# The recurrent stage in chunks of 64 tokens instead of 32, each solved over two 32-token halves

## The chip, the cores and the metric

The kernel runs on one core of one Trainium2 chip. The metric is the device time of one execution in microseconds (us); below it is the median of the runs shown. The engines are named as in the profile: PE (TensorE matmul), PEld (its weight load), DVE (VectorE), ACT (ScalarE), POOL (GpSimd) and SP (SyncE, which here issues loads).

## The reference, cut to what matters

The kernel computes one step of a hybrid decoder layer for a prompt of 2048 tokens and a small sample. Only the recurrence of its RWKV-7 branch for the prompt bears on the change: eight heads, each with a 64 x 64 state `s` that every token reads and rewrites.

```
def step(s, inp):
    r_t, w_t, k_t, v_t, kk_t, kka_t = inp
    s_kk = einsum('bhvk,bhk->bhv', s, kk_t)
    s = s * w_t[:, :, None, :] - s_kk[..., None] * kka_t[:, :, None, :] + v_t[..., None] * k_t[:, :, None, :]
    return s, einsum('bhvk,bhk->bhv', s, r_t)
s_final, ys = lax.scan(step, s0, xs)          # over the tokens
y = (y - mean) * rsqrt(var + eps) * lnx_g + lnx_b   # per head, and a bonus term and a gate behind it
```

Within a chunk of tokens the scan is solved in closed form: with products between the chunk's keys (the grams, masked to a triangle), the corrections u of all its tokens solve a unit triangular system, so that u is an inverse times a right-hand side q. Then the state moves on by one chunk, and the outputs y come from the state and from the grams.

## The kernel before, in words

Stages run one after another: the front, a sample start, the attention of the prompt and of the sample, `stage_rwkv` (L979), the merge. The change is in `stage_rwkv`, apart from constant masks made in the front.

The stage walks over 16 blocks of 128 tokens in a software pipeline. In round n each engine does, for different blocks: the recurrence of block n, the inverses of block n+1 (grams L1323, then five rounds of squaring L1346), the features of block n+2 (decays, keys, transposes), the inputs of block n+3, and the normalisation and output of block n-1. The order of each engine's work in a round is written out by hand, and semaphores tie the engines to one another.

A block has four chunks of 32 tokens. Heads are spread over the array in pairs: the four 32-row and 32-column tiles of TensorE each hold the tokens of one pair p, and e picks one of its two heads. For each chunk:

- `open_chunk` (L1349): gram times v (L1359), state times keys (L1363) into q, half of keys times values (L1368). It waits for the copy of the y before it, since q and y lie in the same PSUM tile.
- ACT copies q (`take_q`, L1588); `solve` (L1372): the other half of keys times values (L1377), inverse times q (L1385).
- DVE copies u (`take_u`, L1796); `close_chunk` (L1389): rates times u into the state (L1396, L1405), the state's part of y (L1400), the grams' parts of y (L1410, L1414).
- DVE adds the new state (`next_state`, L1804); ACT copies y (`take_y`, L1595).

Between these, PE does the other blocks' work: grams, `low_rank` (L1255, L1256), squares, transposes (`turn_values` L1278, `turn_keys` L1287, `turn_rates` L1294, `norms` L1272, `turn_y` L1310), `bonus_sums` (L1301), `key_sums` (L1265). On ACT the decays need two activation tables, so in every round a block stands there without a break: a table load, two roots, a table load, the exponentials, and three copies out of PSUM (L1550 to L1568). On DVE the norm's `centre_y` (L1818) reads two operands from SBUF; `mask` (L1764) writes the masked grams. On POOL `first_product` (L1176) adds the identity to the triangle, `shifted` (L1157) multiplies the token differences, `receptance` (L1190) forms the operand of the bonus sums.

Of the kernel before, what the change touches and what calls it, by code (L numbers as in the profile page):

```python
# [22 lines left out]
P = 128  # L23
# [137 lines left out]
def stage_front(nc, t, k, h_t, z_t, z_s, w_idx, w_idx_s, scores, part):  # L161
# [3 lines left out]
    with Stage(nc, "fro") as s:  # L165
# [128 lines left out]
        def _(pool):  # L294
# [19 lines left out]
            for c, lt, le, gt in ((32, k.m_lt, k.m_le, k.m_gt), (4, k.s_lt, k.s_le, k.s_gt)):  # L314
# [8 lines left out]
            chain.link(pool.memset(k.chunk_start[:, :].rearrange("p (b c) -> p b c", c=32)[:, :, 0:1], 0.0))  # L323
# [655 lines left out]
def stage_rwkv(nc, t, k, z_t, y_t, weights):  # L979


    C = 32
    NC = P // C
    BLK = 2 * NC
    with Stage(nc, "rwk") as s:
# [4 lines left out]
        mask4, eye = s.sb("mask4", [P, 4 * C]), s.sb("eye", [P, C])  # L990
        rheads = s.sb("rheads", [P, 4, P])
        g_tok = s.sb("g_tok", [P, 2, HD])
# [4 lines left out]
        kr, sq, th_w, th_a, mix, cum, kk, rk, bs = (s.sb(n, E) for n in ("kr", "sq", "th_w", "th_a", "mix", "cum", "kk", "rk", "bs"))  # L997
# [7 lines left out]
        v_tok = [s.sb(f"v_tok{i}", [P, NC, 2 * HD]) for i in range(3)]  # L1005
        k_tok = [s.sb(f"k_tok{i}", [P, NC, 2 * HD]) for i in range(2)]
        b_tok = [s.sb(f"b_tok{i}", [P, NC, 2 * HD]) for i in range(2)]
        gram = [s.sb(f"gram{i}", [P, 2, NC, 2, 2, C]) for i in range(2)]
        ta = [s.sb(f"ta{i}", [P, BLK, 2, C]) for i in range(2)]
        pw = [s.sb(f"pw{i}", [P, BLK, C]) for i in range(2)]  # L1010
        inv = [s.sb(f"inv{i}", [P, BLK, C]) for i in range(2)]
        q_tok = [s.sb(f"q_tok{i}", [P, 2, HD]) for i in range(2)]
        u_tok = [s.sb(f"u_tok{i}", [P, 2, HD]) for i in range(2)]
        state = [s.sb(f"state{i}", [P, 2, 2, HD]) for i in range(2)]
        kept = s.sb("kept", [P, 2, 2, HD])
        y_tok = [s.sb(f"y_tok{i}", [P, NC, 2, HD]) for i in range(2)]
        y_sum, y_var = s.sb("y_sum", [P, 8]), s.sb("y_var", [P, 8])
        y_c, y_sq, y_n, y_g = (s.sb(n, [P, 8, HD]) for n in ("y_c", "y_sq", "y_n", "y_g"))
        y_2, g_th, gate, y_out = (s.sb(n, E) for n in ("y_2", "g_th", "gate", "y_out"))
        bias = [s.sb(f"bias{i}", E) for i in range(3)]  # L1020
        s_out = s.sb("s_out", [HD, 4, P])
# [17 lines left out]
        q_ok, q_copied, u_ok, u_copied, o_half, o_ok, st, keep, y_ok, y_copied = (  # L1039
            s.sem(n) for n in ("q_ok", "q_copied", "u_ok", "u_copied", "o_half", "o_ok", "st", "keep", "y_ok", "y_copied"))  # L1040
# [23 lines left out]
        def rows(p):  # L1064
            return slice(C * p, C * p + C)

        def half_of(e):
            return slice(HD * e, HD * e + HD)

        def tokens(c):  # L1070
            return slice(C * c, C * c + C)

        def lower(g):

            return g[:, :, :, 1, 0, :].rearrange("p e c t -> p (e c) t")

        HEADS = [(p, e) for p in range(4) for e in range(2)]
# [6 lines left out]
        def _(sp):  # L1084
# [13 lines left out]
            for m in range(4):  # L1098
# [4 lines left out]
                if m == 0:  # L1103
                    for p in range(4):
                        sp.dma_start(g_tok[rows(p), :, :].rearrange("p e v -> p (e v)"),
                                     t["lnx_g"][:, P * p:P * p + P].to_broadcast([C, P])).then_inc(g_in, 16)
            for n in range(NT):
                sp.wait_ge(u_ok, NC * n + 1)
                if n and n + 3 < NT:
                    load_z(n + 3, 1, Z_PIECES[1][2])  # L1110
                weights.load_piece(sp, 3 * n)
                sp.wait_ge(o_ok, NC * n + 1)
                if n >= 2:
                    sp.wait_ge(gate_ok, n - 1)
                load_gate(n, slice(0, 2))
                sp.wait_ge(u_ok, NC * n + 2)
                load_gate(n, slice(2, 4))
                sp.wait_ge(o_ok, NC * n + 2)
                weights.load_piece(sp, 3 * n + 1)
                if n + 4 < NT:  # L1120
                    free_z(n + 4, 0)
                    load_z(n + 4, 0, Z_PIECES[0][0])
                    sp.wait_ge(u_ok, NC * n + 3)
                    load_z(n + 4, 0, Z_PIECES[0][1])
                    sp.wait_ge(o_ok, NC * n + 3)
                    load_z(n + 4, 0, Z_PIECES[0][2])
                    sp.wait_ge(u_ok, NC * n + 4)
                    free_z(n + 4, 1)
                    load_z(n + 4, 1, Z_PIECES[1][0])
                    sp.wait_ge(o_ok, NC * n + 4)  # L1130
                    load_z(n + 4, 1, Z_PIECES[1][1])
                else:
                    sp.wait_ge(u_ok, NC * n + 4)
# [12 lines left out]
        def _(pool):  # L1146
# [24 lines left out]
            def first_product(m):  # L1171

                pool.wait_ge(masked, 2 * m + 2)
                if m:
                    pool.wait_ge(acc_ok, 4 * m)
                pool.tensor_tensor(ta[1][:, :, 1, :], lower(gram[m % 2]), eye[:, None, :].to_broadcast([P, BLK, C]), ALU.add).then_inc(acc1_ok, 1)  # L1176
# [24 lines left out]
            def scale_y(e):  # L1201
                pool.wait_ge(yn_ok, e + 1)
                if e:
                    pool.wait_ge(y_turned, e)
                pool.tensor_tensor(y_g[:, :, :].rearrange("p (c e) v -> p c (e v)", e=2), y_n[:, :, :].rearrange("p (c e) v -> p c (e v)", e=2),
                                   g_tok[:, :, :].rearrange("p e v -> p (e v)")[:, None, :].to_broadcast([P, NC, P]), ALU.mult).then_inc(yg_ok, 1)

            def put_out(e):
                pool.wait_ge(y2_ok, e + 1)
                pool.wait_ge(gate_ok, e + 1)  # L1210
                if e:
                    pool.wait_ge(stored, 16 * e)
# [5 lines left out]
            for n in ROUNDS:  # L1218
                if there(n):
                    keep_state(n, 0)  # L1220
                if there(n + 1):
                    end_keys(n + 1)
                if there(n + 1):
                    first_product(n + 1)
                if there(n + 3):
                    shifted(n + 3, 0)
# [4 lines left out]
                if there(n):  # L1231
                    keep_state(n, 2)
# [4 lines left out]
                if there(n):  # L1237
                    keep_state(n, 3)
                if there(n + 2):
# [6 lines left out]
        def _(pe):  # L1246
# [28 lines left out]
            def turn_values(m):  # L1275
                pe.wait_ge(thw_ok, m + 1)
                for c in range(NC):
# [1926 lines left out]
```

## Time and profile before

| what | us |
|---|---|
| median of 3 runs | 3555.86 (3547.37 to 3557.55) |
| span of the profiled execution | 3554.5 |
| of it before the stage | 2087.5 |
| of it in the stage, 2087.5 to 2733.0 | 645.5 |
| of it behind the stage | 821.5 |
| PE busy in the stage | 525.4 |
| DVE, ACT, POOL busy in the stage | 339.9, 345.0, 245.7 |
| mean granted TensorE clock in the stage, as a share of full | 0.67 |

The span is the trace's own length; the profiled execution lies 1.4 us under the median of the runs. A granted clock of 1 is 2.4 GHz, of 0.5 it is 1.2 GHz; a share between the two is a mix in time. A row of the timeline names a run of equal instructions, its start, its length and the wait ahead of it; the trace counts two matmuls for each call here, so that a group of 8 calls has x16. Starts of consecutive groups on PE, one taken from the next, give what a group costs, since their modelled ends overlap.

### The profile page before, as it was taken

Reading aid. Unit: us, or ns where it says so; the run is one execution under the profiler, and the core shown is the slowest. Engines: PE = TensorE matmul, PEld = TensorE weight load, DVE = VectorE, ACT = ScalarE, POOL = GpSimd, SP = SyncE. Lnnn points to the kernel's source line nnn. Section 1 sums busy time; section 2 is a strip of 40 time slices with the busy share of each in tenths; the row PEclk is TensorE's granted clock in tenths of the full one; section 3 lists DMA queues with packets and bytes.
Section 4 is the critical chain, followed back from the end, with each engine's and each line's share of the span. In section 5 each row is a group of like instructions: output and inputs, shape, how many; then the busy total and the mean of one; then the engine's idle time right before and its main releaser. Section 6 shows DMA issues by size and latency. Waiting matters only on the chain. (4 is left out here: it accounts for less than half of the span.)

```text
span 3554.5 us, 73586 instructions
## 1 busy us (share of the span) xinstructions
PE 3287.0 (92%) x29368; PEld 1981.7 (56%) x29368; DVE 2139.6 (60%) x4326; ACT 1100.1 (31%) x2345; POOL 525.2 (15%) x764
## 2 busy tenths in 40 slices
PE   8999999999999999699999658888886899999998
PEld 4544445555555555466666437667665555555553
DVE  2018889999999999377766544546553344432211
ACT  4136650000000000255555245555552111111211
POOL 3330000000000000211011333433432000000000
PEclk9999999999999999699999766666776999999999
DMA  5241111111111111332111641222212511121110
GB/s 157 74 106 50 42 46 56 56 56 56 55 61 55 56 56 50 88 80 53 42 37 29 213 122 41 51 48 52 53 28 68 167 63 57 62 75 63 48 39 24
DMA packets 215719, 233.95 MB, mean 66 GB/s; under 512 B 28665, under 2 KB 190900, under 8 KB 214884
## 3 DMA queue, kind: packets, MB, share of 16 engines
q1 hardware_dynamic: 147832, 110.00, 11.4%
q0 software_dynamic: 23696, 59.79, 5.9%
q10 hardware_dynamic: 43868, 59.62, 4.8%
q8 instruction: 232, 3.80, 0.5%
q14 instruction: 91, 0.75, 0.1%
HBM read 158.69 MB, written 70.63 MB: 65 GB/s over the span
## 5 line engine op out<-in xcount | busy, mean ns | idle before, releaser
L409 PE MATMUL fro_acc<-h_t,fro_w 128*128 128x416 f32 x3280 | 1175.0, 516 | 0.0
L409 PEld LDWEIGHTS fro_acc<-h_t,fro_w 128*128 128x128 f32 x3280 | 614.7, 190 | 542.9 <-issue 535.9
L692 DVE TENSOR_SCALAR_CACHE_REDUCE fro_work<-scores,fro_real 128x384 uint8<-128x384 f32 (+6 forms) x462 | 656.2, 1474 | 2.1
L516 ACT ACTIVATE fro_out<-fro_acc 128x416 f32<-128x416 f32 (+3 forms) x230 | 118.1, 513 | 794.0 <-PE fro_acc L409 711.2
L2134 PE MATMUL mrg_po<-mrg_wo,mrg_mrg 128*128 128x512 f32 (+1 forms) x544 | 238.2, 596 | 5.1 <-DVE mrg_mrg L2239 5.1
L3070 DVE CUSTOM_DVE_ANT_0 att_seen<-att_ps,scores 128x512 f32<-128x512 f32 (+3 forms) x320 | 181.4, 608 | 100.8 <-PE att_ps L2956 100.3
L2166 PE MATMUL mrg_pg<-mrg_wg,mrg_x_t 128*128 128x512 f32 (+1 forms) x544 | 236.3, 592 | 0.0
L658 DVE SCALAR_TENSOR_TENSOR scores<-fro_work,w_idx,scores 128x512 f32<-128x512 f32 (+3 forms) x280 | 188.0, 671 | 39.2 <-ACT fro_work L573 12.2
L2134 PEld LDWEIGHTS mrg_po<-mrg_wo,mrg_mrg 128*128 128x128 f32 (+1 forms) x544 | 101.1, 186 | 139.2 <-issue 133.8
L3040 ACT ACTIVATE att_seen<-att_seen,att_shift 128x128 f32<-128x128 f32 (+15 forms) x128 | 152.7, 1195 | 84.1 <-DVE att_shift L3078 84.1
L2956 PE MATMUL att_ps<-att_kt,att_qt 64*128 64x512 f32 (+3 forms) x640 | 159.7, 588 | 14.2 <-POOL att_sel L2927 14.2
L573 ACT ACTIVATE fro_work<-fro_wk 128x512 f32<-128x512 f32 (+3 forms) x320 | 144.5, 539 | 90.8 <-PE fro_wk L482 89.9
L2166 PEld LDWEIGHTS mrg_pg<-mrg_wg,mrg_x_t 128*128 128x128 f32 (+1 forms) x544 | 100.5, 185 | 125.5 <-issue 124.9
L2992 PEld LDWEIGHTS att_po<-att_prob_t,att_v 128*64 128x64 f32 x2176 | 116.9, 137 | 91.3 <-issue 59.4
L2969 PE MATMUL att_pt<-ident,att_seen 128*128 128x128 f32 x1088 | 157.0, 284 | 6.2 <-ACT att_seen L3040 6.0
L2992 PE MATMUL att_po<-att_prob_t,att_v 128*64 128x128 f32 x2176 | 155.3, 282 | 0.0
L2085 POOL DMA_DIRECT2D mrg_m_in<-z_t x72 | 51.2, 711 | 676.3 <-DVE mrg_mrg L2239 673.7
L2444 POOL MEMSET sst_w2a<- 128x1024 f32 x1 | 1.0, 951 | 995.6 <-POOLq L100 995.6
L2101 PE MATMUL mrg_br<-mrg_y_in,wr 128*128 128x256 f32 (+2 forms) x576 | 127.9, 366 | 19.0 <-DMA mrg_y_in<-y_t 14.4
L2314 DVE SCALAR_TENSOR_TENSOR mrg_th<-mrg_th,mrg_pw 128x1024 f32<-128x1024 f32 (+1 forms) x17 | 20.8, 1221 | 204.2 <-ACT mrg_th L2216 204.2
L2329 DVE RECIPROCAL mrg_rstd<-mrg_rstd 128x1 f32<-128x1 f32 (+1 forms) x17 | 2.8, 163 | 225.6 <-ACT mrg_rstd L2202 225.6
L2969 PEld LDWEIGHTS att_pt<-ident,att_seen 128*128 128x128 f32 x1088 | 118.7, 143 | 35.0 <-issue 29.8
(441 smaller groups left out, 4667.4 us busy)
## 6 DMA issues: line engine op xcount, KB each, us to landing
z_t<-fro_out ACTq DMA_DIRECT2D x180, 208.0 KB
fro_w<-in_w_in SPq DMA_DIRECT2D x41, 512.0 KB, 4.1
mrg_m_in<-z_t POOLq DMA_DIRECT2D x56, 256.0 KB, 3.5
scores<-in_cache_kv POOLq DMA_DIRECT2D x108, 128.0 KB, 3.2
rwk_zi<-z_t SPq DMA_DIRECT2D x80, 129.0 KB, 2.6
z_t<-fro_out ACTq DMA_DIRECT2D x45, 192.0 KB
scores<-in_x_prompt SPq DMA_DIRECT2D x16, 512.0 KB, 8.2
mrg_x<-in_x_prompt SPq DMA_DIRECT2D x16, 512.0 KB, 3.6
```

The lines of the kernel that those rows point to most:

```text
L409: last = pe.matmul(acc[e % 2][:, 0:CW], w[block_no % 3][:, kk, :], h_t[:, kk, CW * g:CW * g + CW], start=(kk == 0), stop=(kk == KD - 1))
L573: act.activation(rel[m % 8][:, 0:width], wk[m % 6][:, 0:width], ACT.Relu).then_inc(relued, 1)
L658: ins = dve.scalar_tensor_tensor(o, rel[m % 8][:, 0:width], wh, o, ALU.mult, ALU.add)
L692: chain.mark(dve.tensor_scalar(junk[b % 2][:, 0:n], scores[:, c:c + n], realf[:, b:b + 1], None, op, ALU.add, accum_out=count[:, b:b + 1]))
L2101: last = pe.matmul(br[:, at % 2, W * a:W * a + m], w[:, c, d * P:(d + 1) * P], y_in[g % 2][:, a, c, 0:m], start=(c == 0), stop=(c == 3))
L2134: last = pe.matmul(po[0:n, 512 * h:512 * h + 512], mrg[g % 2][:, c, o:o + n], wo[:, c, 512 * h:512 * h + 512], start=(c == 0), stop=(c == ...
L2166: last = pe.matmul(pg[0:n, 512 * h:512 * h + 512], x_t[:, c, 0:n], wg[:, c, 512 * h:512 * h + 512], start=(c == 0), stop=(c == KD - 1))
L2956: last = pe.matmul(ps[z % 2][e][:, 0:width], qt[b % 2][w, hh, :], kt[w, 512 * sl:512 * sl + width], start=True, stop=True)
L2969: last = pe.transpose(pt[i % 2][:, 256 * e + P * a:256 * e + P * a + P], seen[n % 3][e][:, P * kb:P * kb + P], k.ident[:, :])
L2992: last = pe.matmul(po[b % 2][64 * e:64 * e + 64, P * hh:P * hh + P], v[:, kb, 64 * e:64 * e + 64], prob_t[i % 4][:, 256 * e + P * a:256 * ...
L3040: act.activation(row, row, ACT.Exp, bias=shift[n % 3][:, e:e + 1], scale=scale, accum_out=total[b % 2][:, 4 * e + hh:4 * e + hh + 1]).then ...
L3070: dve.tensor_tensor_reduce(seen[n % 3][e][:, 512 * sl:512 * sl + width], ps[z % 2][e][:, 0:width], scores[:, c:c + width], 1.0, -3.4e38, A ...
```

## The change

A block now has two chunks of 64 tokens. Each chunk's triangular system is solved by forward substitution over two halves of 32 tokens, so that only 32 x 32 inverses are kept: solve the first half, multiply it by the off-diagonal block of the gram (`carry`), add that to the second half's right-hand side, solve the second half. The five rounds of squaring have as many matmuls as before. Groups that were spread over 32-wide tiles now use 64 x 64 tiles, all four of them (state, keys times values, rates times u) or the two on the diagonal (grams times v and u); the two solves and the carry use 32 x 32 tiles, two at a time. The grams come in two parts, one for each chunk, with 128 moving columns each. The gram part of q for the next chunk is issued at the end of `close_chunk` (`begin_q`).

```
-    C = 32
+    C, H = 64, 32
     NC = P // C
-    BLK = 2 * NC
+    BLK = 2 * NC * 2
...
             def first_product(m):
...
+                for i, (x, h) in enumerate(FOURTHS):
+                    w = fourth(x, h)
+                    pool.tensor_tensor(ta[1][w, :, 1, :], lower(gram[m % 2])[w, :, sub(h)], eye[w, None, :].to_broadcast([H, BLK, H]), ALU.add)\
+                        .then_inc(acc1_ok, 1)
+                    pool.wait_ge(acc1_ok, 4 * m + i + 1)
...
+            def grams(m, c):
...
+                for i in range(2):
+                    for p2, x, e in HEADS:
+                        p = 2 * p2 + x
+                        last = pe.matmul(zz[half_of(x), e, 256 * p2 + P * i:256 * p2 + P * i + P], kbz[half_of(e), i, p, tokens(c)],
+                                         ar[m % 3][half_of(e), p, c, :, :].rearrange("p a c -> p (a c)"), start=True, stop=True)
...
+            def solve(n, c, h):
...
+                for p2, e, x in ALONG:
+                    w = fourth(x, h)
+                    last = pe.matmul(qy[w, e, P + 64 * p2:P + 64 * p2 + 64], inv[n % 2][w, block_no(e, c, p2), :],
+                                     q_tok[m % 2][w, e, p2, :], start=False, stop=True, skip_group_check=True)
                 last.then_inc(u_ok, 1)
+            def carry(n, c):
+                m = NC * n + c
+                pe.wait_ge(u_copied, 4 * m + 2)
+                for p2, e, x in ALONG:
+                    w = fourth(x, 0)
+                    last = pe.matmul(qy[fourth(x, 1), e, 64 * p2:64 * p2 + 64], lower(gram[n % 2])[w, block_no(e, c, p2), sub(1)],
+                                     u_tok[m % 2][w, e, p2, :], start=False, stop=True, skip_group_check=True)
+                last.then_inc(carried, 1)
+            def take_in(n, c):
+                m = NC * n + c
+                now, u = state[m % 2], u_tok[m % 2]
+                pe.wait_ge(u_copied, 4 * m + 4)
...
+            def take_carry(n, c):
+                m = NC * n + c
+                act.wait_ge(carried, m + 1)
+                for x in range(2):
+                    w = fourth(x, 1)
+                    act.activation(q_tok[m % 2][w, :, :, :].rearrange("p e b v -> p e (b v)"), qy[w, :, 0:P], ACT.Copy).then_inc(q_copied, 1)
...
+            def take_u(n, c, h):
...
+                for x in range(2):
+                    w = fourth(x, h)
+                    dve.tensor_copy(u_tok[m % 2][w, :, :, :].rearrange("p e b v -> p e (b v)"), qy[w, :, P:2 * P]).then_inc(u_copied, 1)
...
                 if norm:
                     sum_y(n - 1)
+                    centre_y(n - 1)
+                if inverse:
+                    mask(n + 1, 0)
                 if loop:
-                    take_u(n, 0)
+                    take_u(n, 0, 0)
```

Some tiles share memory now (rk with mix, y_n with y_c, y_g with y_sq, the gate with its tanh, y_out with y_2), with the waits that this asks for, and SP's loads are tied to other semaphores of the recurrence. The new order shows at three places.

On PE, from the close of a block's first chunk to the solve of the next, before (L1346 is the squares, L1363 state times keys):

```order
L1396 MATMUL rwk_oo<-rwk_u_tok,rwk_b_tok 64x64 x4
L1400 MATMUL rwk_qy<-rwk_state,rwk_ar 32x64 x8
L1405 MATMUL rwk_oo<-rwk_u_tok,rwk_b_tok 64x64 x4
L1410 MATMUL rwk_qy<-rwk_v_tok,rwk_gram 32x64 x8
L1414 MATMUL rwk_qy<-rwk_u_tok,rwk_gram 32x64 x8
L1359 MATMUL rwk_qy<-rwk_v_tok,rwk_gram 32x64 x8
L1363 MATMUL rwk_qy<-rwk_state,rwk_ar 32x64 x8
L1368 MATMUL rwk_oo<-rwk_v_tok,rwk_k_tok 64x64 x4
L1346 MATMUL rwk_zz<-rwk_gram,rwk_pw 32x32 x32
L1377 MATMUL rwk_oo<-rwk_v_tok,rwk_k_tok 64x64 x4
L1385 MATMUL rwk_qy<-rwk_q_tok,rwk_inv 32x64 x8
```

The same place after (L1423 to L1427 is `take_in`, L1435 to L1372 `close_chunk` with `begin_q`, L1386 and L1392 `open_chunk`, L1363 the squares, L1405 a half's solve, L1291 and L1300 transposes):

```order
L1291 MATMUL rwk_xx<-ident,rwk_vx 128x128 x4
L1423 MATMUL rwk_oo<-rwk_u_tok,rwk_b_tok 64x64 x8
L1427 MATMUL rwk_qy<-rwk_state,rwk_ar 64x64 x8
L1363 MATMUL rwk_zz<-rwk_gram,rwk_pw 32x32 x32
L1435 MATMUL rwk_qy<-rwk_v_tok,rwk_gram 64x64 x8
L1438 MATMUL rwk_qy<-rwk_u_tok,rwk_gram 64x64 x8
L1372 MATMUL rwk_qy<-rwk_v_tok,rwk_gram 64x64 x8
L1386 MATMUL rwk_qy<-rwk_state,rwk_ar 64x64 x8
L1392 MATMUL rwk_oo<-rwk_v_tok,rwk_k_tok 64x64 x8
L1363 MATMUL rwk_zz<-rwk_ta,rwk_pw 32x64 x32
L1405 MATMUL rwk_qy<-rwk_q_tok,rwk_inv 32x64 x8
L1300 MATMUL rwk_xx<-ident,rwk_kbt 128x128 x4
```

One group of the open (L1372, the gram part of q) has moved ahead of the place where it waits for the copy of y, and the square that stood between open and solve has a successor there; the state's groups stand ahead of the first square. On DVE, the start of a round before:

```order
L1811 TENSOR_REDUCE rwk_y_sum<-rwk_y_tok 128x8
L1796 COPY rwk_u_tok<-rwk_qy 128x128
L1764 TENSOR_TENSOR rwk_gram<-rwk_zz,rwk_mask 128x512 x2
L1804 TENSOR_TENSOR rwk_state<-rwk_oo,rwk_kept 128x256
L1772 STREAM_TRANSPOSE rwk_pw<-rwk_gram 128x256
L1818 SCALAR_TENSOR_TENSOR rwk_y_c<-rwk_y_sum,rwk_y_tok 128x512
L1796 COPY rwk_u_tok<-rwk_qy 128x128
L1707 TENSOR_SCALAR rwk_th_w<-rwk_th_w 128x512
```

and after (L1852 and L1858 are the norm's sum and `centre_y`, L1799 the mask, L1837 the copies of u):

```order
L1852 TENSOR_REDUCE rwk_y_sum<-rwk_y_tok 128x8
L1858 SCALAR_TENSOR_TENSOR rwk_y_c<-rwk_y_sum,rwk_y_tok 128x512
L1799 TENSOR_TENSOR rwk_gram<-rwk_zz,rwk_mask 128x512 x2
L1837 COPY rwk_u_tok<-rwk_qy 32x256 x2
L1799 TENSOR_TENSOR rwk_gram<-rwk_zz,rwk_mask 128x512 x2
L1837 COPY rwk_u_tok<-rwk_qy 32x256 x2
L1807 STREAM_TRANSPOSE rwk_pw<-rwk_gram 128x512
L1845 TENSOR_TENSOR rwk_state<-rwk_oo,rwk_kept 128x256
```

`centre_y` has moved from behind the first state to ahead of the masks and of all copies of u. On ACT, from the second table load on, before:

```order
L1541 ACT_TABLE_LOAD
L1541 ACTIVATE rwk_e_in<-rwk_cum 128x16x32
L1542 ACTIVATE rwk_e_neg<-rwk_cum 128x512
L1546 ACTIVATE rwk_p_end<-rwk_cum 128x16
L1556 ACTIVATE rwk_rnb<-rwk_nrm 128x512
L1562 ACTIVATE rwk_v_tok<-rwk_xx 128x512
L1568 ACTIVATE rwk_k_tok<-rwk_xx 128x512
L1595 ACTIVATE rwk_y_tok<-rwk_qy 128x128
L1576 ACTIVATE rwk_ta<-rwk_zz 128x8x32
L1588 ACTIVATE rwk_q_tok<-rwk_qy 128x128
```

and after (L1607 copies a square, L1626 is `take_carry`):

```order
L1572 ACT_TABLE_LOAD
L1572 ACTIVATE rwk_e_in<-rwk_cum 128x8x64
L1573 ACTIVATE rwk_e_neg<-rwk_cum 128x512
L1577 ACTIVATE rwk_p_end<-rwk_cum 128x8
L1587 ACTIVATE rwk_rnb<-rwk_nrm 128x512
L1593 ACTIVATE rwk_v_tok<-rwk_xx 128x512
L1607 ACTIVATE rwk_ta<-rwk_zz 128x8x32
L1599 ACTIVATE rwk_k_tok<-rwk_xx 128x512
L1626 ACTIVATE rwk_q_tok<-rwk_qy 32x256 x2
```

A copy of y and one of q stood behind the block; now the two copies of the carried half do.

## Rows read from the trace of the kernel before

**Rows 1.** Windows: length, busy PE PEld DVE ACT POOL, PEclk, DMA

```profile
2149.59:2701.59 552.00, 475.58 (x15136) 379.46 (x15135) 297.23 (x562) 295.33 (x796) 214.79 (x214) 0.70 0.18 44
2336.68:2375.45 38.77, 34.01 (x1020) 27.25 (x1016) 19.36 (x41) 21.01 (x57) 15.49 (x15) 0.65 0.21 50
2375.45:2411.59 36.14, 29.79 (x1020) 23.96 (x1016) 19.27 (x40) 20.88 (x57) 15.65 (x15) 0.76 0.22 53
```

**Rows 2.** Timeline of PE, lower level: start, length, work, idle before

```profile
2460.63 0.65 PE L1359 MATMUL rwk_qy<-rwk_v_tok,rwk_gram 32*32 32x64 f32 x16 [0.40 <-ACT rwk_y_tok L1595]
...
2462.02 1.08 PE L1346 MATMUL rwk_zz<-rwk_gram,rwk_pw 32*32 32x32 f32 x64
2463.03 0.49 PE L1377 MATMUL rwk_oo<-rwk_v_tok,rwk_k_tok 32*64 32x64 f32 x8
2463.45 0.65 PE L1385 MATMUL rwk_qy<-rwk_q_tok,rwk_inv 32*32 32x64 f32 x16
2464.03 1.11 PE L1278 MATMUL rwk_xx<-ident,rwk_vx 128*128 128x128 f32 x4
...
2466.17 0.49 PE L1396 MATMUL rwk_oo<-rwk_u_tok,rwk_b_tok 32*64 32x64 f32 x8
...
2467.41 0.65 PE L1410 MATMUL rwk_qy<-rwk_v_tok,rwk_gram 32*32 32x64 f32 x16
...
2468.26 1.81 PE L1346 MATMUL rwk_zz<-rwk_ta,rwk_pw 32*32 32x64 f32 x64
```

**Rows 3.** Timeline of PE, upper level; two groups behind a long wait

```profile
2447.00 0.34 PE L1396 MATMUL rwk_oo<-rwk_u_tok,rwk_b_tok 32*64 32x64 f32 x8
...
2448.29 0.76 PE L1346 MATMUL rwk_zz<-rwk_ta,rwk_pw 32*32 32x32 f32 x64
...
2643.12 0.43 PE L1359 MATMUL rwk_qy<-rwk_v_tok,rwk_gram 32*32 32x64 f32 x16 [0.40 <-ACT rwk_y_tok L1595]
...
2644.02 0.37 PE L1346 MATMUL rwk_zz<-rwk_gram,rwk_pw 32*32 32x32 f32 x19
...
2645.84 0.34 PE L1377 MATMUL rwk_oo<-rwk_v_tok,rwk_k_tok 32*64 32x64 f32 x8
...
2646.47 0.66 PE L1278 MATMUL rwk_xx<-ident,rwk_vx 128*128 128x128 f32 x4
...
2653.69 0.43 PE L1359 MATMUL rwk_qy<-rwk_v_tok,rwk_gram 32*32 32x64 f32 x16 [3.12 <-ACT rwk_y_tok L1595]
...
2654.43 0.49 PE L1368 MATMUL rwk_oo<-rwk_v_tok,rwk_k_tok 32*64 32x64 f32 x8
```

**Rows 4.** Waits of 2150:2720: total us, times, longest us

```profile
PE rwk_qy L1359 <- ACT rwk_y_tok L1595: 32.0, 32, 3.1
...
PE rwk_zz L1323 <- DVE rwk_nrm L1718: 9.0, 12, 1.1
...
PE rwk_xx L1287 <- issue: 8.6, 5, 3.4
...
PE rwk_oo L1377 <- issue: 0.7, 1, 0.7
```

**Rows 5.** Timeline of ACT: block of table loads, copies behind it

```profile
2426.44 1.28 ACT L1550 ACT_TABLE_LOAD   x1
...
2431.14 0.57 ACT L1562 ACTIVATE rwk_v_tok<-rwk_xx 128x512 f32<-128x512 f32 x1
...
2432.09 0.27 ACT L1595 ACTIVATE rwk_y_tok<-rwk_qy 128x128 f32<-128x128 f32 x1
```

**Rows 6.** DVE: lines L1818, L2530 (min/median/max ns); timeline

```profile
L1818 DVE SCALAR_TENSOR_TENSOR rwk_y_c<-rwk_y_sum,rwk_y_tok x16: 682/1530/5040, 2192.1 to 2723.3; 128x512 f32<-128x512 f32 x16
...
L2530 DVE COPY sst_tok<-sst_pb x3: 679/679/679, 1474.0 to 1477.1; 32x512 f32<-32x512 f32 x3
...
2459.99 3.37 DVE L1818 SCALAR_TENSOR_TENSOR rwk_y_c<-rwk_y_sum,rwk_y_tok 128x512 f32<-128x512 f32 x1
```

**Rows 7.** Timeline of POOL beside that centre_y

```profile
2459.12 1.67 POOL L1157 TENSOR_TENSOR rwk_pm<-rwk_zi,param 128x896 f32<-128x896 f32 x1
```

More of the change, by code:

```diff
@@ L1222, in _ @@
                     end_keys(n + 1)
+                if there(n + 3):
+                    shifted(n + 3, 0)
                 if there(n + 1):
                     first_product(n + 1)
[L1225 to L1226 removed]
                 if there(n):
@@ L1349, in open_chunk @@
             def open_chunk(n, c):
                 m = NC * n + c
-                g, now = gram[n % 2], state[c % 2]
-                if c == 0:
-                    pe.wait_ge(v_ok, n + 1)
-                    pe.wait_ge(b_ok, n + 1)
                 if m:
                     pe.wait_ge(y_copied, m)
-                for e in range(2):
-                    for p in range(4):
-                        pe.matmul(qy[rows(p), e, 0:64], g[rows(p), e, c, 0, 0, :], v_tok[n % 3][rows(p), c, half_of(e)], start=True, stop=False,
-                                  skip_group_check=True)
+                else:
+                    begin_q(0, 0).then_inc(y_ok, 1)
+                    pe.wait_ge(y_ok, 1)
@@ L1389, in close_chunk @@
             def close_chunk(n, c):
                 m = NC * n + c
-                g, now, u = gram[n % 2], state[c % 2], u_tok[m % 2]
-                pe.wait_ge(u_copied, m + 1)
-                pe.wait_ge(o_half, 3 * m + 2)
-                for p in (0, 1):
-                    for e in range(2):
-                        last = pe.matmul(oo[half_of(e), p % 2, 0:64], b_tok[n % 2][rows(p), c, half_of(e)], u[rows(p), e, :],
-                                         start=False, stop=True, skip_group_check=True)
@@ L1407, in close_chunk @@
[L1407 to L1415 removed]
+                pe.wait_ge(r_half, m + 1)
@@ L1424, in _ @@
                 if inverse:
-                    grams(n + 1)
+                    grams(n + 1, 0)
                 if loop:
-                    solve(n, 0)
+                    solve(n, 0, 0)
                 if features:
@@ L1430, in _ @@
                 if loop:
-                    close_chunk(n, 0)
-                    open_chunk(n, 1)
+                    carry(n, 0)
+                if inverse:
+                    grams(n + 1, 1)
+                if loop:
+                    solve(n, 0, 1)
+                if features:
+                    turn_values(n + 2)
+                if loop:
+                    take_in(n, 0)
                 if inverse:
@@ L1435, in _ @@
                 if loop:
-                    solve(n, 1)
-                if features:
-                    turn_values(n + 2)
+                    close_chunk(n, 0)
+                if loop:
+                    open_chunk(n, 1)
+                if inverse:
+                    square(n + 1, 1)
+                if loop:
+                    solve(n, 1, 0)
                 if inverse:
                     turn_keys(n + 1)
+                if features:
+                    norms(n + 2)
+                if loop:
+                    carry(n, 1)
+                if inverse:
+                    square(n + 1, 2)
+                if loop:
+                    solve(n, 1, 1)
+                if inverse:
+                    turn_rates(n + 1)
+                if inverse:
+                    square(n + 1, 3)
+                if loop:
+                    take_in(n, 1)
+                if features:
+                    bonus_sums(n + 2)
                 if loop:
```

413 lines of the change are left out of this document (191 added, 222 removed).

## The prediction

> **What bounds the kernel now.** Only the recurrent stage changes. I read the windows first: in fifteen rounds PE is busy for 475.6 of 552.0 us, DVE for 297, ACT for 295, POOL for 215 [rows 1]. A round is 36.8 us, of which PE is busy for 31.7; so PE bounds the stage, and what matters is its work, the level of its clock, and what it waits for. The clock decides as much as the work: a round of 38.77 us had a mean granted clock of 0.65, one of 36.14 us with the same number of matmuls had 0.76 [rows 1], so that a tenth of clock is worth about 2.4 us a round. Over the fifteen rounds the share was 0.70, a mix of the two levels, 1.2 and 2.4 GHz.
>
> Then the waits. PE stood still for 76.4 us in those rounds, 5.1 a round. The largest part is 32.0 us for the copy of y at the opening of a chunk, up to 3.1 us at a time, and 9.0 us at the grams [rows 4]; with the small ones it makes some 47 us, 3.1 a round. Seven rows of "issue", from 8.6 down to 0.7 us [rows 4], sum to 31.0 us, 2.1 a round.
>
> **PE's work in the chunks.** Costs go from start to start. At the lower level an open costs 2462.02 - 2460.63 = 1.39 us, a solve 2464.03 - 2463.03 = 1.00, a close 2468.26 - 2466.17 = 2.09 [rows 2]: 4.48, and 17.9 for four chunks. At the upper level these are 0.90, 0.63 and 1.29 [rows 3]: 2.82, and 11.3.
>
> No 64 x 64 tile is in this trace, so I build the new price from passes. The two y groups of the close take 2468.26 - 2467.41 = 0.85 us, that is 0.43 for 16 matmuls on four tiles, four deep: 0.107 us for one matmul of 64 columns. The square agrees: 64 on four tiles in 1.81, 16 deep [rows 2]. A group that is followed by another tile shape costs 0.15 more: the 16 of L1385 take 0.58 [rows 2]. A chunk now has ten groups of 16. Four lie on all four quadrants (4 deep, 0.43), six on two tiles (8 deep, 0.86): 4 x 0.43 + 6 x 0.86 = 6.9, and some five changes of shape, 0.75: 7.6 us, 15.2 a round. At the upper level I halve the pass, but keep a group of four tiles at 0.25 and a change at 0.10: 4 x 0.25 + 6 x 0.46 + 0.5 = 4.3, 8.6 a round. The chunks save 2.7 us a round at either level.
>
> The two parts of the grams issue 64 matmuls of 128 columns on four tiles, 16 deep at 0.214 us: 3.4, with two changes 3.7, against 16 x 0.107 + 0.15 = 1.9 before, where eight tiles worked: 1.8 us more, at the upper level 0.6 to 1.0 more. Squares keep their 160 calls. At the mix of levels in before PE's work falls by **1.4 us a round**. Bounds: if the quadrants go only two at a time, eight groups grow by 0.43 and the sum is +2.0; if neighbouring two-tile groups overlap where their tiles differ, as the solves and the squares might, half of twelve groups shrink by 0.43 and it is -4.0. I take the middle, because the 8 matmuls of L1377, which lie on two row and two column groups, take only 0.42 with their change of shape [rows 2], which is nearer to four at a time than to two.
>
> **Issue.** These waits sit behind dense runs of small matmuls. There are a quarter fewer of them now (some 756 a round instead of 1,012, by the calls in the code), and each one streams longer. Between nothing and the whole 2.1 us I take **-1.2 us a round**.
>
> **The new waits.** Forward substitution puts two hand-overs into a chunk where there was one: u copied by DVE, carry, q copied by ACT, solve, u copied again. Each copy is two instructions on 32 partitions. No such tile of 256 elements was in before; 32 partitions with 512 took 679 ns [rows 6], as long as 128 would, so I take 0.42 for 256, between 0.30 and 0.52: 0.84 a pair. Place by place, for the mix of levels:
> - The second chunk's open stands right behind the close and waits for a copy of 512 elements, 0.57 [rows 5], with its signal 0.75.
> - ACT's block lasts 2432.09 - 2426.44 = 5.65 us [rows 5]. Before, the third open waited for the y copy behind it. Now `norms` and the second `carry` stand there: the norms' operand is ready some 4.8 us after the block's start, and PE has a square (1.8), a solve (0.9) and four transposes (1.0) to do, 3.7 in all at the lower level and 2.1 at the upper: a wait of 1.0 to 2.7. The carry then waits for u, which DVE copies only behind the power that needs a square copied at the block's end: 1.5. Together 3.0.
> - `take_in` of the first chunk waits for a pair of copies, 0.84, with four transposes beside them: 0.5.
> - Bonus sums and key sums keep their feeding chains on DVE, POOL and ACT, while PE arrives sooner: 1.0 and 0.9.
> - The first carry: `centre_y` and a mask stand ahead of u's copy now, with `low_rank` on PE as cover: 0.4.
>
> That is 6.6 us a round against 3.1: **+3.5**, with 4.5 and 9 as ends. Edits priced at nothing: POOL's `first_product` in four steps with waits of their own has half the elements of a `shifted` (1.67 us for 896 [rows 7]) in all its steps together, some 2 us, and the close and open ahead of square 1 cover it; if that cover is gone it costs 0.7 a round. The transposes of 512 instead of 256 elements, the shared tiles and SP's new semaphores lie beside PE's work; late loads would show at the gate or at `shifted`, each of which has a round in hand.
>
> **The clock.** At the same clock the sum would be -1.4 - 1.2 + 3.5 = +0.9 us a round, a loss. What turns it is the level. In before it rose where PE worked without a pause through wide matmuls: behind bonus sums and transposes a whole close ran in 1.29 us [rows 3]. It fell behind the long waits: after one of 3.12 us the open began at the upper level, and its third group already took 0.49 instead of the 0.34 that a group of that tile takes at the upper level [rows 3]. Now the longest waits are split into shorter ones, and a chunk is fewer, longer streams with 10 shape changes a round instead of about 32. I expect a share of 0.78 instead of 0.70, which at 2.4 us a tenth is **-1.9 us a round**. This is the least certain term, between +1.2 (0.65) and -3.0.
>
> **Sum.** -1.4 - 1.2 + 3.5 - 1.9 = -1.0 a round, -16 over sixteen rounds. Filling and draining the pipeline, where the longer grams and the two-step chunk stand alone, costs some 2. The profiled execution of 3554.5 us lies 1.4 under the median, so I add to the median: 3555.9 - 14 = **3541**.
>
> **Rivals.**
> 1. The clock does not rise. More and longer gaps at norms, carry and bonus sums reset it as the 3.12 us wait did. At 0.70 the sum is 0.9 x 16 + 2 = +16: 3572; at 0.65, 1.2 a round more, 3591. It decides from 0.74 on downward (0.9 - 1.0). For it speaks that PE waits twice as long in all; against it that the single waits are shorter than 3.1. The Trainium skill, page "TensorE: Matmul & The Clock Gate", section "HAM oscillation — how this bites in real kernels", says that idle gaps between bursts of matmuls put the clock back each time; the row of the 3.12 us wait agrees, and by that rule this rival, not the forecast, would hold, with its 3572 to 3591.
> 2. `centre_y`, now ahead of u's first copy, becomes the hand-over that PE waits for. It took 682 ns at best, 1,530 in the median and 5,040 at worst; in the timeline one took 3.37 us, beside POOL work that began before it [rows 6, 7]. At a round's start POOL has the bias and output products to do. At 3.4 us instead of 1.5 the first carry waits 2 us more: 3541 + 32 = 3573; it decides above about 2 us. The Trainium skill, page "Advanced Engine Details and Errata", section "GPSIMD Details", says that POOL shares a read and a write interface with DVE, and that DVE instructions with two SBUF inputs conflict with it; the spread of 682 to 5,040 ns agrees.
> 3. Better than forecast: copies of 0.30 and two-tile groups that overlap, together 2 us a round: 3509.
> 4. The waits take the whole gain, as one that was hidden on ACT appears on PE: 3555.
>
> **Chances.** Forecast 0.38, its own range 3528 to 3556; rivals 0.22, 0.10, 0.20 and 0.10. A measurement of this kernel tells apart about 0.3%, 10.7 us. Faster than 3545.2: rival 3 and two thirds of the forecast, 0.45. Within it: the rest of the forecast and rival 4, 0.22. Slower than 3566.5: rivals 1 and 2, 0.33 with rounding. The range of 8 in 10 goes from rival 3 to rival 1 at 0.65: 3503 to 3592.
>
> **What would show it.** In the new profile: a round of 35.8 us; PE's groups on 64 x 64 quadrants at about 0.43 us at the lower level; issue under 1 us a round; waits of 6 to 7 us a round, with norms and the second carry first; a share of 0.78. A share at or below 0.72 is rival 1; a `centre_y` above 2 us and a first carry that waits over 2 us is rival 2; groups of 0.86 on four quadrants would break the work term.

## The result

The changed kernel took 3572.35 us (3569.54 to 3579.35) where the kernel before took 3553.3: a ratio of 1.0059, 95% interval 1.0043 to 1.0075. It is slower, by 19 us between the medians and by some 21 us by the ratio; the forecast was 14 us faster. The profiled execution of after has a span of 3576.2 us, 21.7 more than before's: 2.7 up to the first recurrent round, 12.0 in the fifteen rounds, 3.0 from there to the end of the stage, and 4.0 in the merge, which the change does not touch.

The windows view of after, one row for the fifteen rounds (length, busy us of PE, PEld, DVE, ACT and POOL with their counts, granted clock, DMA), answers to the first of [rows 1]:

```profile
2152.33:2716.30 563.97, 422.06 (x11304) 364.33 (x11296) 339.26 (x621) 307.26 (x795) 241.73 (x227) 0.76 0.17 43
```

PE is busy for 53.5 us less than before, and its clock's share rose from 0.70 to 0.76; but it stands still for 563.97 - 422.06 = 141.9 us instead of 76.4. The idle time ate the gain and 12 us more. The waits view of after, of the same rounds (total us, times, longest), against [rows 4]:

```profile
PE rwk_qy L1414 <- DVE rwk_u_tok L1837: 31.6, 23, 3.3
PE rwk_zz L1285 <- ACT rwk_rnb L1587: 31.5, 14, 2.9
PE rwk_xx L1314 <- POOL rwk_mix L1211: 19.6, 14, 2.5
PE rwk_zz L1278 <- ACT rwk_sq L1540: 15.7, 13, 1.8
PE rwk_zz L1363 <- DVE rwk_ta L1824: 11.7, 15, 1.1
PE rwk_oo L1423 <- DVE rwk_u_tok L1837: 9.4, 15, 1.3
PE rwk_qy L1386 <- ACT rwk_y_tok L1633: 7.3, 15, 0.5
PE rwk_zz L1363 <- POOL rwk_ta L1195: 6.4, 6, 1.4
PE rwk_xx L1291 <- ACT rwk_th_w L1547: 4.0, 9, 0.4
PE rwk_zz L1363 <- issue: 2.3, 4, 0.9
PE rwk_zz L1339 <- issue: 0.5, 1, 0.5
```

The first two are the carries (L1414, of both chunks) and the norms (L1285). By the timeline, 24.0 us of the first row stand at the carry of the second chunk, most of them 1.66 us long. One place in the timelines shows how they hang together. ACT's block starts at 2430.46; the norms' operand is written from 2434.63, and the copy of a square at 2435.63:

```profile
2430.46 1.28 ACT L1581 ACT_TABLE_LOAD   x1
...
2434.63 0.61 ACT L1587 ACTIVATE rwk_rnb<-rwk_nrm 128x512 f32<-128x512 f32 x1
...
2435.63 0.37 ACT L1607 ACTIVATE rwk_ta<-rwk_zz 128x256 f32<-128x256 f32 x1
```

DVE, which works in its written order, waits 3.64 us for that square, and only then, behind a transpose and an addition, copies the u of the second chunk's first half. PE had solved for that u by about 2432.2 (L1405, the first row of PE further down):

```profile
2436.03 0.45 DVE L1816 STREAM_TRANSPOSE rwk_pw<-rwk_ta 128x256 f32<-128x256 f32 x1 [3.64 <-ACT rwk_ta L1607]
2436.40 0.38 DVE L1824 TENSOR_TENSOR rwk_ta<-rwk_zz,rwk_ta 128x256 f32<-128x256 f32 x1
2436.71 0.85 DVE L1837 COPY rwk_u_tok<-rwk_qy 32x256 f32<-32x256 f32 x2
```

Between the end of the keys' transposes (L1300), at 2432.81, and the carry (L1414), at 2437.61, PE does only the four transposes of the norms, in 4.8 us:

```profile
2431.58 0.64 PE L1405 MATMUL rwk_qy<-rwk_q_tok,rwk_inv 32*32 32x64 f32 x16
2432.15 0.66 PE L1300 MATMUL rwk_xx<-ident,rwk_kbt 128*128 128x128 f32 x4
2435.30 0.65 PE L1285 MATMUL rwk_zz<-ident,rwk_rnb 128*128 128x128 f32 x4 [2.49 <-ACT rwk_rnb L1587]
2437.61 0.74 PE L1414 MATMUL rwk_qy<-rwk_u_tok,rwk_gram 32*32 32x64 f32 x10 [1.66 <-DVE rwk_u_tok L1837]
```

### The profile page after: what moved, and what is told of

Same layout as the page of the kernel before. It is cut to its first block and busy times, and to the rows that moved or that the text cites. A ratio compares the mean times of both kernels' runs of the same rounds, so it can differ in the third digit from the quotient of the medians.

```text
span 3576.2 us, 65310 instructions
## 1 busy us (share of the span) xinstructions
PE 3227.2 (90%) x25272; PEld 1964.1 (55%) x25272; DVE 2183.8 (61%) x4382; ACT 1112.8 (31%) x2345; POOL 553.5 (15%) x780
```

## The experiments

All ratios are to the kernel before, with 95% intervals. That kernel was run again beside each group of experiments (medians 3548.9 to 3554.3); after was not, so differences of a few microseconds to after, or between runs of different groups, mean little. "Share" is the mean granted clock of the fifteen rounds as a share of full, pauses included. "Idle" is the length of the fifteen rounds less PE's busy time in them. Busy time falls with a higher clock at the same work, so the two columns separate waits from clock.

| run | median us | ratio | share | PE busy | PE idle |
|---|---|---|---|---|---|
| before | 3553.3 | 1 | 0.70 | 475.6 | 76.4 |
| after | 3572.35 | 1.0059 (1.0043 to 1.0075) | 0.76 | 422.1 | 141.9 |
| norms_early | 3586.38 | 1.0094 (1.0067 to 1.0122) | 0.75 | 423.5 | 143.7 |
| u_early | 3522.27 | 0.9904 (0.9874 to 0.9935) | 0.83 | 393.9 | 117.7 |
| chain_first | 3585.41 | 1.0113 (1.0073 to 1.0153) | 0.81 | 393.3 | 147.8 |
| keys_early | 3559.19 | 1.0017 (0.9995 to 1.004) | 0.82 | 394.5 | 147.6 |
| u_dve | 3529.18 | 0.9911 (0.988 to 0.9941) | 0.86 | 384.9 | 130.9 |
| u_pe | 3576.32 | 1.0065 (1.0044 to 1.0086) | 0.82 | 406.2 | 153.2 |
| centre_back | 3564.94 | 1.0024 (1.0002 to 1.0045) | 0.76 | 418.0 | 134.8 |
| copy_u | 3490.48 | 0.9829 (0.981 to 0.9848) | 0.86 | 380.7 | 93.1 |
| mix1 | 3473.13 | 0.9759 (0.9728 to 0.979) | 0.91 | 359.7 | 104.0 |
| mix3 | 3494.55 | 0.9848 (0.9808 to 0.9889) | 0.84 | 385.7 | 90.3 |
| noroot_after | 3527.8 | 0.993 (0.9909 to 0.9951) | 0.82 | 390.2 | 122.0 |
| noroot_before | 3511.74 | 0.9882 (0.9862 to 0.9903) | 0.78 | 436.8 | 66.7 |
| fill_after | 3569.58 | 1.0051 (1.0031 to 1.007) | 0.79 | 416.4 | 139.2 |
| fill_before | 3530.84 | 0.9946 (0.9927 to 0.9965) | 0.80 | 450.7 | 70.5 |
| mix1_fill | 3475.89 | 0.9785 (0.9756 to 0.9814) | 0.93 | 364.6 | 94.4 |
| mix1_fillk | 3474.75 | 0.9782 (0.9755 to 0.9809) | 0.93 | 363.1 | 98.2 |

The share and the two columns are of one profiled execution each, and that is not always a typical one: chain_first's took 3556 us where its median is 3585, u_dve's 3537 where its median is 3529. Single rounds of one kernel differ in their share by up to 0.3, so a few microseconds there mean nothing.

**Which of the two pauses, and whose order.** Three edits of after's orders.

norms_early, on ACT:

```
-                    exps(n + 2)
                     spread_norms(n + 2)
+                    exps(n + 2)
```

> The kernel after, with ACT's spread of the norms ahead of the three exponentials of its block. Theory A (after is held by the chain of hand-overs of the second chunk, which runs through ACT's block as a whole): the wait at the norms, 31.5 us in fifteen rounds, falls below 10, but the second carry still needs a u that DVE copies behind a power fed from the end of the block, so its wait grows by about as much and the time stays at 3572 within 6 us. Rival B (each wait on PE is a loss by itself): 31 us less, 3541.

Measured 3586. The norms' wait fell from 31.5 to 3.5 us and the carries' rose from 31.6 to 66.1; together they did not shrink but grew by 6.5. Taking away one wait alone gave nothing, as theory A says, and rival B falls. The median lies 14 us above after, more than expected; in the profile the rounds took 567.2 us against 564.0, so most of it is outside the rounds or differs from run to run.

u_early, on DVE (the copy of u ahead of the power) and on PE (the carry ahead of the norms):

```
+                if loop:
+                    take_u(n, 1, 0)
                 if inverse:
                     power(n + 1, 1)
-                if loop:
-                    take_u(n, 1, 0)
...
+                if loop:
+                    carry(n, 1)
                 if features:
                     norms(n + 2)
-                if loop:
-                    carry(n, 1)
```

> The kernel after, with DVE's first copy of u in the second chunk ahead of the power that waits for ACT's block, and PE's carry ahead of the norms. Theory A: the carry's wait (two thirds of 35.9 us, some 24) goes, but the copy of the carried half on ACT still stands behind the block, so the second solve waits instead; 0.5 to 1.2 us a round, 3554 to 3564. Rival B: all of the 24 us, 3548. Rival C (PE's work and clock hold the round, waits are slack): 3572.

Measured 3522, 50 us under after and faster than before; all three forecasts were higher. The window row of its fifteen rounds:

```profile
2155.63:2667.20 511.57, 393.86 (x11304) 338.74 (x11296) 339.66 (x621) 307.52 (x796) 241.12 (x227) 0.83 0.19 47
```

Idle time fell by 24.2 us, what rival B gave; but busy time fell by 28.2 as well, at the same number of matmuls, because the share went from 0.76 to 0.83. No theory had that half.

> The kernel after, with only DVE's first copy of u in the second chunk moved ahead of the power that waits for ACT's block; PE's order is as in after, so that the norms come first and then the carry. Theory A (DVE's order is what costs): PE's carry finds its u when the norms are done, the carry's wait goes and the time is that of u_early, 3522 within 8. Rival D (u_early gained because PE's pause was cut in two by a carry between): the norms' pause stays whole, the clock stays near 0.76, and only the 24 us of wait are saved, 3548.

> The kernel after, with only PE's second carry moved ahead of the norms; DVE still copies u behind the power. Theory A: the carry now takes the whole pause in one piece, some 4.2 us, and the norms follow without a wait; the sum of waits stays within 5 us of after, and the time is 3572 to 3590, as with norms_early, where the same two pauses fell together. Rival D (PE's order alone gives part of u_early's gain): 3550 or less.

u_dve has only the DVE move, u_pe only PE's. Measured 3529 and 3576: DVE's order does it, PE's gives nothing, and rival D falls for both. So the cost lies in one line of DVE's order: the copy of u stands behind a power that waits for ACT's block. How it costs is another matter than theory A has it. In u_dve's profile the carries' wait fell from 31.6 to 10.1 us, but PE's idle time is only 11.0 us under after's, since waits for POOL grew (at the bonus sums from 19.6 to 28.4 us, at square 1 from 6.4 to 12.4); its busy time is 37.2 us lower, at the same matmuls, through the clock.

chain_first has u_dve's edit and takes the hand-overs out of ACT's block besides (only ACT's part is printed):

```
+                    spread_norms(n + 2)
+                if inverse:
+                    take_square(n + 1, 1)
+                if loop:
+                    take_carry(n, 1)
+                if features:
                     exps(n + 2)
-                    spread_norms(n + 2)
                     take_values(n + 2)
```

> The kernel after, with the hand-overs of the second chunk taken out of ACT's block: the spread of the norms, the copy of a square and the carried half stand ahead of the second table load and the exponentials, and DVE copies u ahead of the power. Theory A: the norms and the second carry stop waiting (2.1 and some 1.6 us a round), a square waits a little more; 2.5 to 3.5 us a round less, 3520 to 3535, and so faster than the kernel before (3553). Rival C (PE's work and clock hold the round): 3572 within 6.

It missed: 3585, with runs from 3556 to 3606, and 56 us above u_dve, so the part on ACT lost all that DVE's part gained. In its trace, which is of the fastest of its runs, the norms' wait fell to 1.7 us and the carries' to 9.0, and a new one came: the exponentials now wait behind the carried half, the block ends later, and with it the copy of the keys, which PE's next transposes need. The squares wait longer for DVE too. From the waits of chain_first:

```profile
PE rwk_xx L1307 <- ACT rwk_k_tok L1599: 39.0, 14, 3.0
PE rwk_zz L1363 <- DVE rwk_ta L1826: 28.4, 26, 2.0
```

keys_early puts ACT's raw keys ahead of the copy of y:

```
-                if loop:
-                    take_y(n, 1)
                 if inputs:
                     squash(n + 3)
                     raw_keys(n + 3)
+                if loop:
+                    take_y(n, 1)
```

> The kernel after, with ACT's raw keys of a later block ahead of its copy of the second chunk's y. The wait of the key sums (15.7 us) should go. Theory A, if this wait is a loss of its own: 1.0 us a round, 3557. Rival: the next round's first copies of u and the grams wait instead, since the norm's sums on DVE start no earlier: 3572.

3559, near theory A's number, but not by its reason: the key sums' wait went from 15.7 us to 1.1 and the grams waited 17.5 us for DVE instead, as the rival has it, so that idle time rose to 147.6; the gain is all in busy time, with the share at 0.82.

**The block itself.**

```
-                act.activation(nrm[:, :], nrm[:, :], ACT.Sqrt).then_inc(rooted, 1)
+                act.activation(nrm[:, :], nrm[:, :], ACT.Identity).then_inc(rooted, 1)
```

and the same for `deviation`, in both kernels. These kernels leave out the stage's two square roots, and two table loads a round go with them.

> The kernel after with ACT's two square roots of the stage left out (a plain copy in their place, so that ACT needs no second activation table there and the two table loads of 1.28 us a round fall away; the norms and the variances are then not rooted). Theory A (ACT's block feeds the second chunk's pauses): the norms' and the second carry's waits, some 4 us a round together, shrink by about 2.5: 33 us at least, 3540 or less, more if the clock follows. Rival C: 3572 within 6.

> The kernel before with the same two square roots left out. There one copy of y stands behind ACT's block, and PE waits for it 1 to 3 us a round; by theory A this shrinks by 0.5 to 1.5 us a round: 3532 to 3548, so that the block cost the new order more than the old one. Rival C: 3554 within 6.

After fell to 3528, by 45 us, as theory A has it, but before fell to 3512, by 41 us where 5 to 21 were expected: idle time fell by 10 and the share rose to 0.78. So two table loads cost the two orders about the same, and the part of theory A by which the block weighs more on the new order falls. What is new is what stands behind the block on DVE (u_dve).

**The hand-overs and the norm.** In centre_back `centre_y` goes back behind the first state.

> The kernel after, with the norm's centre_y on DVE moved back behind the first state. If centre_y ahead of u's first copy were the cause (a rival of the prediction), the first carry's wait (about 0.4 to 0.8 us a round) would go and some 10 us with it, 3562 or less. By theory A it changes little, 3572 within 6, since the second chunk's pauses remain.

3565: 7 us by the medians, 12 by the ratios, whose intervals still overlap; that lies between the two forecasts. What one `centre_y` took in after tells more (line view, min/median/max ns, against the first of [rows 6]):

```profile
L1858 DVE SCALAR_TENSOR_TENSOR rwk_y_c<-rwk_y_sum,rwk_y_tok x16: 693/1180/1332, 2190.4 to 2740.9; 128x512 f32<-128x512 f32 x16
```

It never took above 1.33 us there, and the long executions of before are gone.

copy_u is u_early with each hand-over in one instruction (and the same on ACT; only the first copy of all stays in two); mix1 has in addition `first_product` ahead of the shifts on POOL, without its wait for them.

```
-                for x in range(2):
-                    w = fourth(x, h)
-                    dve.tensor_copy(u_tok[m % 2][w, :, :, :]..., qy[w, :, P:2 * P]).then_inc(u_copied, 1)
+                    dve.tensor_copy(u_tok[m % 2][:, :, :, :]..., qy[:, :, P:2 * P]).then_inc(u_copied, 2)
...
+                if there(n + 1):
+                    first_product(n + 1)
                 if there(n + 3):
                     shifted(n + 3, 0)
-                if there(n + 1):
-                    first_product(n + 1)
```

> u_early, with each hand-over copied by one instruction over all partitions instead of two over 32 each (0.42 us less per hand-over of u and of the carried half), and POOL's first_product ahead of its product of shifts. Theory A (the chain of hand-overs holds the round): each round has six such pairs, of which three or four stand on PE's path, 1.2 to 1.6 us, and square 1 stops waiting, 0.4: 1.5 to 2 us a round less than u_early, 3490 to 3500. Rival C (PE's work holds the round now): 3522 within 6.

> u_early with the hand-overs copied by one instruction over all partitions, and POOL's first_product left where it is. Between u_early (about 3524) and the run that had both edits (3473) lie some 50 us, twice what I had expected. Theory E (the pairs of copies on 32 partitions are the larger loss, on PE's path at nearly every hand-over): 40 us of it come here, 3476 to 3490. Rival F (the place of first_product does it): 3505 or more.

mix1 ran 3473, 2.4% under before and 49 us under u_early where 22 to 32 were expected; copy_u 3490, so that theory E holds for some 32 of these 49 us (27 of 52 by the ratios) and the place of `first_product` is worth the rest. Lines of copy_u (the first) and of after give the sizes: a copy of u over 128 partitions takes 415 ns in the median, one over 32 partitions 417 in the mean, and the four steps of `first_product` take 3.4 us together:

```profile
L1838 DVE COPY rwk_u_tok<-rwk_qy x63: 405/415/425, 2160.7 to 2643.1; 128x256 f32<-128x256 f32 x63
...
L1837 DVE COPY rwk_u_tok<-rwk_qy 32x256 f32<-32x256 f32 x128 | 53.4, 417 | 8.0 <-PE rwk_qy L1405 5.1
...
L1195 POOL TENSOR_TENSOR rwk_ta<-rwk_gram,rwk_eye 32x256 f32<-32x256 f32 x60 | 50.5, 842 | 16.6 <-DVE rwk_gram L1799 11.7 <-POOL rwk_pm L1170 1.4
```

mix3 adds to mix1 the edits of keys_early and centre_back.

> The run with u_early's order, whole copies and the early first_product, and in addition ACT's raw keys ahead of the copy of y and the norm's centre_y behind the first state. The key sums' wait of 16.7 us should go; where the grams do not wait instead, 8 to 16 us less than 3473: 3457 to 3465. Rival: the wait moves to the grams, as it did when the raw keys were moved alone: 3473 within 6.

3495: both were good alone and together they do not pay on top. The wait moved to the grams (16.3 us), as the rival has it, but the time is 21 us above mix1 and not within 6. Idle time is the lowest of the kernels in the new order, 90.3 us, and yet the run is slower than mix1: busy time is 26 us higher at the same matmuls, with a share of 0.84 instead of 0.91.

**The pauses and the clock.** These put useless matmuls right ahead of a pause.

```
-                for j in range(GR):
+                for j in [*range(GR), *range(GR)]:
                     last = pe.transpose(xx[:, 1, P * j:P * j + P], kbt[:, 0, j // 2, ...
```

and in before the second round of squares likewise. mix1_fillk is mix1 with the edit above; mix1_fill doubles the transposes of y too.

> The kernel after, with the four transposes of the keys, which stand right ahead of the norms' pause, done twice into the same place: 0.6 to 1.0 us a round of useless work on PE inside a pause of 2.1. Theory G (pauses of PE pull the clock down): the share rises from 0.76 to 0.80 or more, and although PE does more the time falls by 10 to 25 us, 3547 to 3562. Rival H (the share follows from the rest of the round): the share stays within 0.02, the time is 3572 within 6, or up to 10 us more where the transposes outlast the pause.

> The kernel before, with the second round of squares, which stands right ahead of the pause for the copy of y behind ACT's block, done twice into the same place: 1.0 to 1.9 us a round of useless work against a pause of 1.1 to 3.1. Theory G: the share rises from 0.70 to 0.74 or more; the pause takes up most of the work, and the time is 3530 to 3550. Rival H: the share stays, and what outlasts the pause is added, 3555 to 3565.

> The fastest order so far (3473, share 0.91), with the transposes of the keys and those of y done twice each; the first stand ahead of the second carry and the norms' pause of 1.3 us a round, the second ahead of the key sums' pause of 1.1. Theory G: the share rises to 0.95 or more, worth about 10 us, less the 0.3 us a round that the carry comes later: 3465 to 3473. Rival H: 5 to 12 us more, 3478 to 3485.

> The same fastest order with only the transposes of the keys done twice. Theory G: share 0.93 or more, 3468 to 3476. Rival H: 3475 to 3482. Between the two runs the doubled transposes of y are seen by themselves.

The kernel before, with about a thousand matmuls more, is faster, 3531 against 3553; its window row:

```profile
2149.76:2671.04 521.28, 450.74 (x16095) 363.59 (x16094) 301.96 (x562) 294.11 (x795) 215.94 (x215) 0.80 0.19 47
```

Its wait for y fell from 30.8 to 13.2 us in the rounds, but waits for issue rose from 31 to 41, so that idle time fell only from 76.4 to 70.5; the rest, 25 us of busy time in spite of the added work, goes with the share of 0.80. Time and share are those of theory G. Whether the filled pause raised the share, or the added dense work by itself, is not told apart. In after the same trick raised the share to 0.79 only and the time stayed, as rival H has it; the transposes fill less than a third of a pause that comes in two pieces. In mix1 both ways gave a share of 0.93 and left the time where it was (3475 and 3476 against 3473), between the two forecasts or at their edge: idle time fell by 6 to 10 us, and busy time rose by 3 to 5 with the added work.

## Why the prediction was wrong, step by step

- **PE's work: right, as far as single groups show it.** In after at the lower level, the timeline gives 0.48 and 0.43 us for the groups on four quadrants, 1.86 for a part of the grams, and about 0.9 for the two-tile groups of the close (0.43, 3.7 for both parts, and 0.86 were forecast):

```profile
2417.00 0.70 PE L1386 MATMUL rwk_qy<-rwk_state,rwk_ar 64*64 64x64 f32 x16
2417.48 0.65 PE L1392 MATMUL rwk_oo<-rwk_v_tok,rwk_k_tok 64*64 64x64 f32 x16
2417.91 1.93 PE L1339 MATMUL rwk_zz<-rwk_ar,rwk_kbz 64*64 64x128 f32 x32
2419.77 0.72 PE L1405 MATMUL rwk_qy<-rwk_q_tok,rwk_inv 32*32 32x64 f32 x16
...
2448.87 1.12 PE L1435 MATMUL rwk_qy<-rwk_v_tok,rwk_gram 64*64 64x64 f32 x16
2449.78 1.06 PE L1438 MATMUL rwk_qy<-rwk_u_tok,rwk_gram 64*64 64x64 f32 x16
2450.64 0.67 PE L1372 MATMUL rwk_qy<-rwk_v_tok,rwk_gram 64*64 64x64 f32 x16
```

- **The clock: nearly right.** A share of 0.78 was forecast and 0.76 came. Work and clock together were to save 3.3 us of busy time a round; they saved 53.5 / 15 = 3.6.
- **Issue: right and larger.** 31.0 us fell to 2.8, 1.9 a round instead of 1.2.
- **The new waits: this term failed.** Forecast were 6.6 us a round, with 4.5 and 9 as ends; the rows above, without the two of issue, sum to 137 us, 9.2 a round. The norms and the second carry were priced at 3.0 and are 3.7; bonus and key sums at 1.9 and are 2.4; `take_in` and the open were 1.2 and are 1.1; the first carry was 0.4 and is 0.5. What was missing altogether is 1.5 a round at places that the step had not listed or had priced at nothing: square 3 behind DVE's power (11.7 us), square 1 behind POOL's `first_product` (6.4; the step took 2 us for it, it takes 3.4 and waits besides), the transposes of the values (4.0). Against 3.1 before that is +6.1 a round instead of +3.5, and with the other terms as forecast (-1.4, -1.2, -1.9) already a loss of 1.6. The experiments show a second fault in the term: it priced a wait by the time that PE stands still. The copy of u behind the power was seen and put at 1.5 us a round; taking it from there (u_dve) gave 43 us, some 2.7 a round, and in the profile three quarters of it was busy time. Waits and clock were added as if each stood by itself, and they do not.
- **Idle time as a whole** was to rise by 3.5 - 1.2 = 2.3 us a round and rose by (141.9 - 76.4) / 15 = 4.4. With 3.6 saved that is the 0.8 by which a round grew, 12 us.
- **Filling and draining** were 2 and are 5.7 in the stage, with the sixteenth round's growth in it: the last round shows the bare two-step chain, with waits of 2.3 and 2.0 us at the carries and 0.9 to 1.0 at the copies around them. The 4.0 us of the merge were not forecast; 2.7 of them stand at one wait of PE for DVE (7.3 us instead of 4.6), and why it grew was not looked into.

Rival 1 gave 3572 and the time came out there, but by luck and not by its mechanism: it had the clock stay at 0.70 or below, and the clock rose. Its ground, that pauses pull the clock down, has some support in the kernel before (fill_before) and less in after (fill_after). The Trainium skill, page "TensorE: Matmul & The Clock Gate", section "HAM oscillation — how this bites in real kernels", describes idle gaps between bursts of matmuls that put the clock back each time. The share that goes from 0.70 to 0.80 in fill_before agrees in its direction; after and keys_early, with 0.76 at 141.9 us idle and 0.82 at 147.6, show that the amount of idle time does not settle it here. Rival 2, `centre_y`, cost some 7 to 12 us, not 32, and not by long executions. Rival 3 needed copies of 0.30 us, and copies of 32 partitions took the 0.42 of the forecast; that cheaper hand-overs pay is what copy_u shows. Rival 4 is nearest in its mechanism, waits that take the whole gain, part of them behind ACT's block, but they took some 20 us more than the gain.

What stays open is the share itself. It is not explained by the sum of the pauses (keys_early and after: 147.6 and 141.9 us idle, shares of 0.82 and 0.76), nor by the longest one (u_pe has one pause of up to 5.2 us a round and 0.82; norms_early one of up to 4.2 and 0.75). Part of this lies in the measure, since the share counts the pauses too: in after the level was still 1.0 through the pause of 2.49 us that begins at 2432.81, fell to 0.5 at about 2437.5, after the second pause, and came back at about 2450.7. The windows view in steps of 0.5 us says more. In after, u_early and u_dve the level fell about as often, some 28 times in the fifteen rounds, but PE spent 271, 175 and 147 us at the lower level, and stood still for 36, 16 and 8 us of that. So these orders differ in how soon the level came back, more than in how often it fell; that waits inside such a stretch make it longer fits these numbers, but no edit tested it. The clock is worth 28 to 37 us between these kernels. It is also open why the doubled transposes helped so little in after.

## What to carry to other kernels

When a dependent step is split in two, price each hand-over on every engine that it crosses, in that engine's written order: what stands ahead of the copy there, and what that in turn waits for, decides more than the copy's own length. Here one copy that stood behind a wait for another engine's block cost 43 us (50 with the carry moved as well), while PE's whole busy time had fallen by 53.5, and moving it by one place made the new order faster than the old. Do not price such a wait by PE's idle time alone: most of what it cost showed as busy time at the lower clock. A copy over a quarter of the partitions took as long as one over all of them (417 and 415 ns), so a hand-over of pieces is best copied whole.

## What the runs showed of the hardware that was not expected

- Useless matmuls ahead of a pause made the kernel before 22 us faster, with the granted clock's share going from 0.70 to 0.80.
- A copy of 256 columns took as long over 32 partitions as over 128, and joining the pairs of copies (copy_u) gave some 30 us.
- Waits for issue on PE fell from 31.0 to 2.8 us when 15,136 matmul records became 11,304, far more than in proportion.
- Two loads of an activation table a round, 2.57 us in sum, cost the kernel before 41 us by the medians, about what they last in sixteen rounds. In the profiled executions the fifteen rounds are 48.5 us shorter without them, and only 9.7 us of that is idle time of PE; the rest is busy time, with the share at 0.78 instead of 0.70.
